# Projecting the next unit's q, k and v between the attention steps of the current one

## The reference

```python
h = _rmsnorm(x, norm_mix)
proj = h @ w_in                                  # (L, 1024) @ (1024, 3072)
na_q, na_k, na_v, d_q, d_k, d_v = jnp.split(proj, splits, axis=-1)
na_out = _neighbourhood_attention(...)           # 8 heads of 64, 8x16 neighbourhood + meta tokens
dq, dk = _rotary(d_q, cos, sin), _rotary(d_k, cos, sin)
diff_out = _diff_attention(...)                  # 4 heads: (softmax(q1 k1) - lam softmax(q2 k2)) v
x = x + jnp.concatenate([na_out, diff_out], axis=-1) @ w_out
x = x + _expert_choice_ffn(_rmsnorm(x, norm_ffn), ...)
```

## Time and profile before

| | us |
|---|---|
| median of 3 runs | 3730.12 |
| lowest, highest | 3727.12, 3762.46 |
| profiled execution, its span | 3762.46, 3762.4 |
| PE busy | 3445.7 (92%) |
| DVE busy | 1943.0 (52%) |
| ACT busy | 1565.1 (42%) |
| projection's matmuls (L1273), three groups together | 812.6 |

### The profile page before, as it was taken

How to read it: one execution, slowest core, us unless ns; L and a number is a source line. 1 busy time by engine, 2 the same in 40 slices (tenths; PEclk the granted TensorE clock), 3 DMA queues, 4 the chain that set the end, 5 groups by cost and what they waited for, 6 DMA issues and landing times.

```text
span 3762.4 us, 55013 instructions
## 1 busy us (share of the span) xinstructions
PE 3445.7 (92%) x20241; PEld 3124.6 (83%) x20241; DVE 1943.0 (52%) x3186; ACT 1565.1 (42%) x2503; POOL 163.6 (4%) x177
## 2 busy tenths in 40 slices
PE   4999999999998988796399999999999999999993
PEld 4878787878786776674399999999999999999993
DVE  4221212132636547224667666676666766666763
ACT  3221212121314224121256555565555565555652
POOL 1000000000000000100000000000000000000001
PEclk8758585756989999897699999999999999999997
DMA  4101010101010011331477777777777777777875
GB/s 131 33 11 32 1 42 1 42 1 34 9 43 25 17 26 46 112 125 45 141 228 244 221 230 233 226 240 224 233 232 225 238 236 222 231 233 229 240 214 177
DMA packets 605125, 514.49 MB, mean 137 GB/s; under 512 B 21080, under 2 KB 583384, under 8 KB 605048
## 3 DMA queue, kind: packets, MB, share of 16 engines
q1 hardware_dynamic: 596856, 487.70, 41.5%
q0 software_dynamic: 8192, 25.70, 3.4%
HBM read 466.56 MB, written 40.86 MB: 135 GB/s over the span
## 4 chain that ended last, share of the span: by engine, by line
PE 54%; issue 40%; DVE 3%; DMA 2%; POOL 1%; ACT 1%; SPq 0%; ACTq 0%; DVEq 0%; POOLq 0%
PE ps L1536 33%; PE ps L1537 15%; PE ps L1463 4%; DMA xt<-x_all_dram 1%; PE ps L1581 1%; DVE top_i L1125 1%; DVE top_v L1123 1%; DVE aff L1126 1%; PE ps L1530 1%; DMA raw<-w_up_dram 0%; DMA y_dram<-yo 0%; POOL rstd L1595 0%; PE ps L1481 0%; DVE mixT_lo L1053 0%; POOL rstd_d L1595 0%
## 5 line engine op out<-in xcount | busy, mean ns | idle before, releaser
L1536 PE MATMUL ps<-xe,w_hi 128*128 128x392 f32 x4096 | 1195.6, 364 | 12.0 <-DVE xe L1168 8.6
L1537 PE MATMUL ps<-xe,w_lo 128*128 128x196 f32 x4096 | 1034.1, 252 | 0.0
L1155 DVE TENSOR_TENSOR w_lo<-raw,w_hi 128x2048 fp32r<-128x2048 f32 x384 | 875.3, 2283 | 11.7 <-ACT w_hi L538 11.7
L1537 PEld LDWEIGHTS ps<-xe,w_lo 128*128 128x128 f32 x4096 | 783.9, 191 | 0.0
L1536 PEld LDWEIGHTS ps<-xe,w_hi 128*128 128x128 f32 x4096 | 769.9, 188 | 15.9 <-issue 15.9
L538 ACT ACTIVATE w_hi<-raw 128x2048 fp32r<-128x2048 f32 x384 | 732.1, 1911 | 85.8 <-DMA raw<-w_gate_dram 75.8
L1536 PE MATMUL ps<-hid,w_hi 128*128 128x392 f32 x2048 | 609.4, 366 | 0.0
L1537 PE MATMUL ps<-hid,w_lo 128*128 128x196 f32 x2048 | 516.8, 252 | 0.0
L1537 PEld LDWEIGHTS ps<-hid,w_lo 128*128 128x128 f32 x2048 | 391.4, 191 | 0.0
L1536 PEld LDWEIGHTS ps<-hid,w_hi 128*128 128x128 f32 x2048 | 384.5, 188 | 0.0
L1188 DVE TENSOR_TENSOR gusum<-ps,part 128x392 f32<-128x392 f32 x256 | 144.9, 566 | 390.4 <-ACT part L538 390.4
(11 more groups left out here) (168 smaller groups left out, 3855.7 us busy)
## 6 DMA issues: line engine op xcount, KB each, us to landing
raw<-w_gate_dram SPq DMA_DIRECT2D x128, 1024.0 KB, 5.3
raw<-w_up_dram SPq DMA_DIRECT2D x128, 1024.0 KB, 5.1
raw<-w_down_dram SPq DMA_DIRECT2D x128, 1024.0 KB, 5.1
wqkv<-w_in_dram SPq DMA_DIRECT2D x24, 512.0 KB, 5.1
xt<-x_all_dram SPq DMA_DIRECT2D x12, 512.0 KB, 4.0
mixed_heads<-mix SPq DMA_DIRECT2D x8, 768.0 KB, 3.9
mixs<-mixed_heads SPq DMA_DIRECT2D x12, 512.0 KB, 4.7
xr<-x_all_dram SPq DMA_DIRECT2D x12, 512.0 KB, 4.2
```

The costliest lines, as they stand in the source:

```text
L1155: dve.tensor_tensor(w_lo[:, n % NW, :], raw[:, n % NRAW, :], w_hi[:, n % NW, :].bitcast(f32), ALU.subtract).then_inc(lo_done, 1)
L1536: pe.matmul(out, w_hi[:, slot, cols], x.rearrange("p h n -> p (h n)"), start=first, stop=False)
L1537: return pe.matmul(out[:, 0:SLOTS], w_lo[:, slot, cols], x[:, 0, :], start=False, stop=last)
```

## The change

- The first unit's projection runs alone, as before. After that, `project(uu, n, half, bank, banks)` emits one half of a chunk. In neighbourhood unit u, step s = 0, 2, ... 22, PE does chunk s/2 of unit u+1 (both halves in a row, 24 matmuls) between the transposes of s-1 and the product of s-2. In differential units 0 to 2, steps 0 to 11 each hold one chunk of the next unit: its first half after the scores, its second after the transposes. The last unit has none.
- `qT` and `kT` have two buffers each. All interleaved chunks use bank 7. The product with v of both kinds moves to bank 6, and it now waits for the `mix` of the step before (before: two steps before, in the neighbourhood steps). In differential units 0 to 2 it comes one step earlier in PE's order: at the end of step s for s-1.
- ACT evacuates a chunk at the head of the next even (or next) step. The weights are laid out by q, k, v, split in six parts of 512 columns, and `wqkv` lies in the memory of `wq_lo`, so a third is loaded once the chunks that use the old one are done.
- `mix` becomes a ring of four tiles. Each step's result is stored by a transfer of its own; DVE waits for the ring's place.
- Rotation is done in eight pieces of 392 columns, one each step, in the unit before: SP issues four swap transfers per piece, DVE multiplies and adds. For differential unit 0 it sits in neighbourhood unit 3.
- In DVE's differential step, the copies of the transposes move behind the scores of the same step. Bias loads of a head are issued at steps 13 and 26. The meta scores alternate between the row halves.
- All unit loops are written out (no hardware loops), and the semaphores count with constants.

```diff
-            def project(uu, before):
-                pe.wait_ge(wq_lo_done, KD * uu + KD + CREDIT)
-                for n, (which, c) in enumerate(CHUNKS):
...
-                    if n >= 2:
-                        pe.wait_ge(pj_evac, NCH * uu + n - 1)
-                    off = (6 + n % 2) * BANK
...
+            def project(uu, n, half, bank, banks):
+                which, c = CHUNKS[n]
+                if half == 0:
+                    pe.wait_ge(wq_lo_done, 6 * uu + 2 * which + 2 + CREDIT)
+                    if n >= banks:
+                        pe.wait_ge(pj_evac, NCH * uu + n - banks + 1)
+                off = bank * BANK
+                cols = slice(c * QCH, (c + 1) * QCH)
+                for k in range(4 * half, 4 * half + 4):
+                    for j, (wt, x) in enumerate(((wq_hi, hT_hi), (wq_hi, hT_lo), (wq_lo, hT_hi))):
+                        ins = pe.matmul(ps[:, off:off + QCH], wt[:, which, k, :], x[:, k, cols],
+                                        start=(k == 0 and j == 0), stop=(k == KD - 1 and j == 2))
...
-                project(u, {(2, 3): first_scores})
-                pe.wait_ge(v_evac, 4 * (u + 1) + CREDIT)
-                for s in range(1, NS + 2):
+                for s in range(NS + 2):
+                    if s == 0:
+                        pe.wait_ge(pj_evac, NCH * u + 8)
+                        pe.wait_ge(na_sb, NS * u + CREDIT)
                     if s < NS:
                         scores(s)
...
+                    if s < 2 * NCH and s % 2 == 0:
+                        for half in range(2):
+                            project(u + 1, s // 2, half, 7, 1)
...
                     if 0 <= s - 2 < NS:
...
-                        if n >= 2:
-                            pe.wait_ge(na_mix, u * NS + n - 1 + CREDIT)
+                        pe.wait_ge(na_mix, u * NS + n + CREDIT)
...
-                        o = ps[0:rows, (6 + b) * BANK:(6 + b) * BANK + DH]
+                        o = ps[0:rows, 6 * BANK:6 * BANK + DH]
...
-                project(u + UNITS, {(2, 2): meta_scores, (2, 3): first_scores})
...
+                for s in range(1, DS + 1 + last):
                     if s < DS:
                         scores(s)
-                    if 0 <= s - 1 < DS:
+                    if not last and s < NCH:
+                        project(UNITS + u + 1, s, 0, 7, 1)
+                    if s - 1 < DS:
...
+                    if not last and s < NCH:
+                        project(UNITS + u + 1, s, 1, 7, 1)
+                    n = s - 1 - last
...
+                dve.wait_ge(swp_in[g % 2], 64 * (g // 2 + 1))
+                own.mark(dve.tensor_tensor(dst[:, cols], dst[:, cols], cos[:, cols], ALU.mult))
+                own.mark(dve.tensor_tensor(swp[:, g % 2, :], swp[:, g % 2, :], sin[:, cols], ALU.mult))
+                own.settle(dve)
+                dve.tensor_tensor(dst[:, cols], dst[:, cols], swp[:, g % 2, :], ALU.add).then_inc(qk_rot, 1)
```

More of the change, by code:

```diff
@@ new lines, in _ @@
+            sp.wait_ge(mask_ready, 1)
+            for a in range(2):
+                load_bias(0, a)
+            for j in range(3):
+                load_w(1, j)
+            for u in range(UNITS):
+                for s in range(NS + 3):
+                    if u == UNITS - 1 and s % 2 and 0 <= (s - 3) // 2 < ROPES:
+                        swap_halves(0, (s - 3) // 2)
+                    if s in (8, 16, 24):
+                        load_w(u + 2, s // 8 - 1)
+                    if s in (13, 26) and u < UNITS - 1:
+                        sp.wait_ge(na_sb, NS * u + s + CREDIT)
+                        load_bias(u + 1, s // 13 - 1)
+                    if s >= 3:
+                        n = s - 3
+                        a, t, rows = NA[n][:3]
+                        g = na_store(u, n)
+                        sp.wait_ge(na_mix, g + 1 + CREDIT)
+                        col = u * P + a * DH
+                        sp.dma_start(mix_d[t * P:t * P + rows, col:col + DH], mix[0:rows, g % MIXR, 0:DH]).then_inc(mix_out[g % MIXR], 16)
@@ L487, in c_stores @@
                 sp.dma_start(h_d[bass.ds(t * P, rows), :], xn2[0:rows, b, :]).then_inc(xn2_out[b], 16)
-            sp.wait_ge(mix_out, 32 * 2 * UNITS + CREDIT)
+            for b in range(MIXR):
+                sp.wait_ge(mix_out[b], 16 * stores(b))
             sp.wait_ge(df_sq, DS * UNITS + CREDIT)
@@ L880, in na_mix_part @@
                 own.settle(dve)
[L881 to L884 removed]
+                g = na_store(u, n)
+                if g >= MIXR:
+                    dve.wait_ge(mix_out[g % MIXR], 16 * (g // MIXR))
+                dve.tensor_scalar(mix[0:rows, g % MIXR, 0:DH], ps[0:rows, 6 * BANK:6 * BANK + DH],
                                   rec[0:rows, n % 4, 0:1], None, ALU.mult).then_inc(na_mix, 1)
[L887 to L890 removed]
+            split_wq(1, 0)
+            split_wq(1, 1)
+            for u in range(UNITS):
                 for s in range(NS + 3):
[L892 to L893 removed]
                     if 0 <= s - 2 < NS:
@@ L1293, in _ @@
             pe.wait_ge(h_ready, NT)
-            with pe.Fori(0, UNITS) as u:
-                pe.wait_ge(na_mix, NS * u + CREDIT)
+            for n in range(NCH):
+                for half in range(2):
+                    project(0, n, half, 6 + n % 2, 2)
+            for u in range(UNITS):
                 def scores(s):
```

422 lines of the change are left out of this document (214 added, 208 removed).

## The result

The changed kernel takes 3771.78 us (median of 4 runs, 3761.9 to 3776.09), the kernel before 3729.11 in the same comparison: ratio 1.013, 95% interval 1.008 to 1.018. It is 1.3% slower; the forecast was 3669. The profiled execution after took 3775.55 us, its span 3773.7.

The account below looks back on a forecast made before the run. PE was taken to bound both kinds of attention unit, the neighbourhood ones at half its clock. Terms of +20, -29 and -52 us, with queues and loops at 0, gave -61 from the median 3730: 3669 us, range 3585 to 3735.

Parts of the forecast that it names:

- Written-out loops: 0, between -8 and +8: All unit loops without hardware loops: no cost in us, at best -8 with branches gone, at worst +8.
- Sum of the attention, -61: Whole attention: +20 us neighbourhood stage, -29 first three differential units, -52 the last one.
- Neighbourhood stage, 851 us: First projection alone 51 us plus four units of 200: +20 us against 830.9, bounds -28 and +104.
- The new wait, 1.1 or 0.6 us in odd steps: Neighbourhood attention: PE's product waits for DVE's scaling, 1.1 us at the fast clock, 0.6 at the slow; even steps covered.
- Differential units 0 to 2, 142 each: Each unit 142 us against a mean of 151.7, about -29 for three; bounds 135 and 151 each.
- Differential unit 3, 101: Last differential unit loses its projection: 101 us, -52 us, bounds -40 and -58.
- Queues, 0: SP's stores, swaps and loads and the weights' split: cost 0, hidden by PE's steps.
- The sum against the median: Whole kernel: the -61 us taken from the median 3730 gives 3669 us; from the profiled 3762, 3701.
- One: Clock stays up in all of neighbourhood attention: stage 699 us, -132, kernel 3517 us; chance 0.08.
- Two: Neighbourhood chunks mostly meet the slow clock after odd-step waits: stage 1003 us, kernel 3821 us; chance 0.11.
- Three: Differential units gain only in the last; the first three stay at 151 us: kernel 3698 us; chance 0.12.
- four: The change's transfers or order hold PE; kernel ends at 3730 us within noise; chance 0.03.

Follow-up runs that it names:

- the run with 24 instructions: Changed kernel plus 24 instructions on PE ahead of the experts, each only counting a semaphore nobody waits for: 3629.99 us, ratio 0.976 to the kernel before.
- the one run whose loop ends 13 instructions into the eighth: Changed kernel plus 160 semaphore-counting instructions on PE ahead of the experts: 3705.54 us (one run).

## Why the prediction was wrong, by its steps

**Written-out loops: 0, between -8 and +8.** This is the step that failed. I priced branches, and not where the loop that stays a loop comes to lie: the diff writes out the units, and the expert loop behind them is still a hardware loop. Writing out the attention loops moved the expert loop on PE from place 20 to place 240 of a block; its price is +142 us, shown by the run with 24 instructions, which gets all of it back. The witness stood in the trace of before: instruction packets in each turn of one loop and none in another.

**Sum of the attention, -61: measured -133 in the profiled executions.** Of the 72 us between them 42 lie in the neighbourhood stage, 23 in differential units 0 to 2 and 7 in unit 3. Its terms:

- *Neighbourhood stage, 851 us: measured 808.8.* The pattern was right: the clock goes up and down once per chunk, mean 0.77. A pair took 14.7 us (162.2 for eleven in the second unit; forecast 15.3), a full unit 191 (200), and the first projection 53 (51).
- *The new wait, 1.1 or 0.6 us in odd steps: measured 46.8 us in 48.* The size was right, the price was not. I took the wait as its own length, and the fall of the clock from the earlier trace rows and an estimate of 3.4 us. The runs showed that the wait makes the clock fall: without it the second unit takes 153.6 us.
- *Differential units 0 to 2, 142 each: measured 136.6, 133.4, 133.3.* With the meta scores grouped they take 142.6, 141.4 and 142.3. So the other terms were right in sum; I kept the 10.71 us of the earlier trace rows for the meta scores, though the diff alternates the row halves. 3.0 to 3.2 us is what they take in the second and third unit, 5.5 in the first, at the slow clock. No row of before showed such an alternation, so the low bound should have been under the 135 us that I gave, which halved the meta scores at most.
- *Differential unit 3, 101: measured 94.1*, the same 7.5 us.
- *Queues, 0: held.* PE waited for no swap and no mix transfer, and the selection stage is unchanged (336.8 and 338.9).

**The sum against the median.** I took a saving worked out on an execution of 3762.46 from a median of 3730. That execution had no neighbourhood unit with the longer fast clock, the median by the levels above has one, worth 33 us, and the changed kernel's runs (3761.9 to 3776.09) show no such levels. So from the median the attention saves 100 us, not 133. The balance: 3729 - 100 + 2 + 142 = 3773, measured 3772. Without the expert loop's shift it is 3631, measured 3630.

**The range.** My own upper bounds add up to +104 - 2 - 40 + 8 = +70, 3800 us. I ended the forecast at 3720 and the range at 3735 without a reason. The measured 3772 lies under 3800, but only by luck: the attention came out at the fast end of its bounds or beyond, and what brought the time up is in none of them.

**The rivals.** *One* (the clock stays up) got 0.08, and its mechanism is right: its stage of 699 us is reached and passed (661 and 637) once the idle in odd steps is gone. By the Trainium skill, "TensorE: Matmul & The Clock Gate", section "Why this matters for your kernels", idle between bursts drops the clock and a busy PE keeps it. In its direction the trace agrees (clock 0.79 with 47.0 us of waits in the stage, 0.92 with 2.3); the waits were 1.5 us at most, shorter than the gaps that the section warns of. What spoke against it was the earlier trace rows, busy 142.19 of 144.50 us at 0.50. What puts the clock down there is not settled; the levels of the kernel before say that a unit of the same instructions can go either way, which the spread of 3727 to 3762 in the times could have told me. *Two* (slower) had the right place, the wait in odd steps, but not the price, 3821 us: pairs stayed at 14.7, far from its 17.4. The change did end on the slower side, by a mechanism that none of the four named. *Three* and *four* are excluded: all differential units gained.

## What to carry to other kernels

A change that writes out loops, or only adds instructions to an engine, moves every loop behind it in that engine's program: look for instruction packets in each turn of a hot loop and "issue" idle at its head, and shift the loop by a few counting instructions if they are there. A wait of 1 us in an engine that bounds the kernel is worth more than its length if the clock falls on it (here three times): look at the granted clock in the microseconds behind it, and move the releasing instruction forward or put independent matmuls in front. And when the runs of a kernel fall into distinct levels, find out which level the profiled execution is, before subtracting from the median.

## What the runs showed of the hardware

- A loop of 1661 instructions on PE returned 14 times without an instruction transfer when it touched seven 16 KB blocks, by the place fitted above, and with 9 transfers a turn when it touched eight, except on three of 14 returns in the one run whose loop ends 13 instructions into the eighth. The gap at its head was 4.0 to 4.7 us; a second one came where the next block began 16 instructions on (1.8 to 3.6 us) or 8 (2.8 to 4.4), and none where it was 76 or 112 away.
- A semaphore-counting instruction took 0.15 us on PE (140 in 20.66 us).
- Scores with few columns cost by the order of their row halves: 52 records of 16 columns took 5.5 us alternating and 10.95 grouped at a granted clock of 0.50. At 1.00 they took 3.0 alternating; no grouped run of them was at 1.00 throughout.
- The same neighbourhood unit, in the same kernel, took 172 to 174 or 206 to 209 us, by how long its clock stayed up.
